# A chunked gated recurrence in 64x64 products: scores and results per 64 tokens, one masked copy for two heads, the state's part one step sooner

## The reference, cut to what matters

```
for each chunk of 64 tokens, each head:
    cum    = cumsum(log_f)                                   # per key channel
    scores[i,j] = sum_d q[i,d] k[j,d] exp(cum[i,d]-cum[j,d]) # j <= i, inside the chunk
    o      = scores @ v + (q * exp(cum)) @ state
    state  = exp(cum[last]) * state + (k * exp(cum[last]-cum))^T @ v
o = rmsnorm(o over the 64 values, norm_g) * silu(g)
```

## Time and profile before

| | |
|---|---|
| Median of 3 runs | 2164.09 us |
| Profiled execution, its own time | 2164.18 us |
| Its span | 2162.5 us |
| TensorE busy | 2140.3 us, 99% |
| VectorE busy | 1239.3 us, 57% |
| ScalarE busy | 914.9 us, 42% |
| GpSimd busy | 138.0 us, 6% |
| Pairs of the recurrence | 226 to 328 us of the span |

### The profile page before, as it was taken

The page is one execution under the profiler, slowest core; times in us unless marked ns, Lnnn a source line. Parts: engine busy times, 40 slices in busy tenths (PEclk is TensorE's granted clock), DMA queues, the critical chain, the costliest instruction groups (busy, mean ns, idle before and its releaser), DMA issues.

```text
span 2162.5 us, 26314 instructions
## 1 busy us (share of the span) xinstructions
PE 2140.3 (99%) x10412; PEld 1696.3 (78%) x10412; DVE 1239.3 (57%) x1835; ACT 914.9 (42%) x1449; POOL 138.0 (6%) x174
## 2 busy tenths in 40 slices
PE   9999999999999999999999999999999999999999
PEld 7768778678888888887777788888887667888887
DVE  5674784564554444474667555555556676555554
ACT  4464444554432332343555433333345555333332
POOL 0000332101000000020011000000021100000000
PEclk9999999999999999999999999999999999999999
DMA  4212112113222223222112222223221112232223
GB/s 175 86 49 88 49 45 93 47 59 127 98 98 98 91 96 106 97 88 88 50 59 68 88 98 98 97 98 98 98 88 59 59 40 89 97 104 96 94 98 107
DMA packets 52105, 187.04 MB, mean 86 GB/s; under 512 B 5904, under 2 KB 6032, under 8 KB 51856
## 3 DMA queue, kind: packets, MB, share of 16 engines
q1 hardware_dynamic: 51840, 185.18, 25.7%
q10 hardware_dynamic: 144, 0.18, 0.0%
HBM read 183.25 MB, written 2.10 MB: 86 GB/s over the span
## 4 chain that ended last, share of the span: by engine, by line
PE 92%; DVE 4%; ACT 2%; issue 1%; DMA 0%; SPq 0%; DVEq 0%; ACTq 0%
PE ps L1016 23%; PE ps L1019 23%; PE ps L1022 23%; PE ps L1040 4%; PE ps L1043 4%; PE ps L1041 4%; PE ps L995 3%; PE ps L1093 1%; PE ps L1145 1%; PE ps L1339 1%; PE ps L1357 1%; PE ps L1117 1%; PE ps L1163 1%; PE ps L1237 1%; DVE wl L1768 1%
## 5 line engine op out<-in xcount | busy, mean ns | idle before, releaser
L1416 ACT CAST wh<-raw 128x1024 fp32r<-128x1024 f32 x334 | 350.9, 1051 | 869.6 <-PE ps L1022 793.0
L1768 DVE TENSOR_TENSOR wl<-raw,wh 128x1024 fp32r<-128x1024 f32 (+2 forms) x338 | 414.7, 1227 | 174.9 <-ACT wh L1416 174.2
L1016 PE MATMUL ps<-hh,wh 128*128 128x512 f32 x1408 | 448.2, 399 | 2.5 <-ACT wh L1422 1.2
L1019 PE MATMUL ps<-hh,wl 128*128 128x512 f32 x1408 | 435.1, 390 | 2.4 <-DVE wl L1768 2.4
L1022 PE MATMUL ps<-hl,wh 128*128 128x512 f32 x1408 | 434.2, 390 | 0.0
L1019 PEld LDWEIGHTS ps<-hh,wl 128*128 128x128 f32 x1408 | 264.1, 188 | 59.6 <-DVE wl L1768 3.7
L1016 PEld LDWEIGHTS ps<-hh,wh 128*128 128x128 f32 x1408 | 257.5, 188 | 67.8 <-issue 15.9
L1022 PEld LDWEIGHTS ps<-hl,wh 128*128 128x128 f32 x1408 | 264.3, 188 | 56.4 <-DVE hl L1849 0.3
L1016 PE MATMUL ps<-R,wh 128*128 128x512 f32 x896 | 286.2, 400 | 0.0
L1019 PE MATMUL ps<-R,wl 128*128 128x512 f32 x896 | 277.4, 390 | 0.5 <-DVE wl L1768 0.5
L1022 PE MATMUL ps<-R,wh 128*128 128x512 f32 x896 | 276.9, 390 | 0.0
(11 more groups left out here) (226 smaller groups left out, 2030.9 us busy)
## 6 DMA issues: line engine op xcount, KB each, us to landing
raw<-in_weights SPq DMA_DIRECT2D x332, 512.0 KB, 3.4
x<-in_x_t SPq DMA_DIRECT2D x4, 512.0 KB, 7.0
F<-in_x_t SPq DMA_DIRECT2D x4, 512.0 KB, 5.0
out<-x SPq DMA_DIRECT2D x8, 256.0 KB, 2.0
raw<-in_weights SPq DMA_DIRECT2D x4, 416.0 KB, 3.2
x<-in_bias SPq DMA_DIRECT2D x1, 1024.0 KB, 7.5
F<-in_weights SPq DMA_DIRECT2D x2, 384.0 KB, 3.8
F<-in_weights SPq DMA_DIRECT2D x2, 256.0 KB, 5.1
```

Of the source, the lines that this page charges most:

```text
L1016: pe.matmul(out, hi[:, k, cs], B.tile(u.src, k)[0], start=k == 0, stop=False)
L1019: pe.matmul(out, lo[:, k, cs], B.tile(u.src, k)[0], start=False, stop=False)
L1416: act.copy(B.wh[s][:, 0:nk * ncol], B.raw[s][:, 0:nk * ncol]).then_inc(S["w_hi"], 1)
L1768: dve.tensor_tensor(lo, src, hi.bitcast(F32), ALU.subtract).then_inc(S[name], 1)
```

## The change

Keys and queries are now of the same 64 tokens. For each chunk c and each head there is one product of the 64 keys (stationary) by 64 queries (level 0) or 32. The even chunk of a pair of chunks goes to output partitions 0 to 63, the odd one to 64 to 127, each head to its bank. Sc shrinks from [2 heads, 512] to [2 heads, 256] columns, the masks to 32 columns, and one copy_predicated takes both heads. Results are products of 64 tokens' values with a 64x64 tile of Sc; even chunks lie in bank 6, odd ones in bank 7, in the first 256 columns. The mean squares go to the last 256 columns of the same two banks, as two products. State's part is a step of its own, `h_carry`, in step 6 behind level 6's scores; it opens the banks, and the results are added to it in step 7. The finishing operations read and write with the chunks' order (even, odd) changed by their patterns. Two constants that nothing used are gone, the first part of the constants is 256 columns smaller, and `h_zero` clears 512 columns and not 1024.

```diff
-CN = ["ident", "onesD", "negU", "negones", "bd64", "ones128"]
+CN = ["ident", "onesD", "bd64", "ones128"]
-NFIRST = 32 + 4 * P
+NFIRST = 32 + 2 * P
...
+                    if lv == 6:
+                        tick.append(("h_carry", p))
...
+    def h_result(self):
+        return self.two_banks(H_OUT[0])[:, :, 0:256]
+    def h_parts(self):
+        return self.V(3).rearrange("p (c t) -> p c t", c=2)
+    def h_squares(self):
+        return self.two_banks(H_OUT[0])[:, :, 256:512]
...
+H_OUT = (6, 7)
...
     def h_score(p, lv):
-            q, k, n = B.f4("F4")[:, p, :], B.f4("F2")[:, p, :], P
+            q, k, n = B.f4("F4")[:, p, :], B.f4("F2")[:, p, :], 64
...
-            q, k, n = B.h_queries(6 * p + lv - 1), B.h_keys(6 * p + lv - 1), 64
-        for tt in range(4):
+            q, k, n = B.h_queries(6 * p + lv - 1), B.h_keys(6 * p + lv - 1), 32
+        for c in range(8):
+            to, ts, qs = slice(64 * (c % 2), 64 * (c % 2) + 64), slice((c // 2) * n, (c // 2) * n + n), slice(c * n, c * n + n)
             for hf in range(2):
-                rr, qs = slice(64 * hf, 64 * hf + 64), slice(tt * n, (tt + 1) * n)
-                last = pe.matmul(two[hf][:, qs], k[rr, tt * P:(tt + 1) * P], q[rr, qs], start=True, stop=True)
+                rr = slice(64 * hf, 64 * hf + 64)
+                last = pe.matmul(two[hf][to, ts], k[rr, c * 64:c * 64 + 64], q[rr, qs], start=c < 2, stop=True,
+                                 skip_group_check=True)
...
+    def h_carry(p):
+        two = [empty(b) for b in H_OUT]
+        state, _ = B.k_state()
         at.wait_ge("hg_st", 7 * (p + 1))
         at.wait_ge("hg_tq", p + 1)
         for c in range(1, 8):
-            cs = slice(c * 64, (c + 1) * 64)
+            cs = slice((c // 2) * 64, (c // 2) * 64 + 64)
             for hf in range(2):
                 rr = slice(64 * hf, 64 * hf + 64)
-                last = pe.matmul(bank[rr, cs], state[rr, c, :], B.V(2)[rr, cs], start=False, stop=True,
+                last = pe.matmul(two[c % 2][rr, cs], state[rr, c, :], B.V(2)[rr, c * 64:(c + 1) * 64], start=c < 3, stop=False,
                                  skip_group_check=True)
+        last.then_inc(S["hg_i"], 1)
+
+    def h_out(p):
...
+        at.wait_ge("hg_i", p + 1)
+        at.wait_ge("hg_c", 7 * (p + 1))
+        for c in range(8):
+            rr, cs = slice(64 * (c % 2), 64 * (c % 2) + 64), slice((c // 2) * 64, (c // 2) * 64 + 64)
+            for hf in range(2):
+                h = 2 * p + hf
+                last = pe.matmul(B.bank[H_OUT[c % 2]][64 * hf:64 * hf + 64, cs], v4[rr, c // 2, h * 64:(h + 1) * 64],
+                                 Sc[rr, hf, c // 2, :], start=False, stop=True, skip_group_check=True)
         last.then_inc(S["hg_o"], 1)
-        emptied[7] = (("hg_d", 2 * p + 1),)
+        for b in H_OUT:
+            emptied[b] = (("hg_d", 2 * p + 1),)

     def h_ms(p):
-        bank = empty(6)
         at.wait_ge("hg_sq", p + 1)
-        pe.matmul(bank[:], B.const("bd64"), B.V(3), start=True, stop=True).then_inc(S["hg_ms"], 1)
-        emptied[6] = (("hg_r", 2 * p + 1),)
+        for i, b in enumerate(H_OUT):
+            last = pe.matmul(B.bank[b][:, 256:512], B.const("bd64"), B.V(3)[:, 256 * i:256 * i + 256], start=True, stop=True)
+            emptied[b] = (("hg_r", 2 * p + 1), ("hg_d", 2 * p + 1))
...
     def h_score(p, lv):                                        # VectorE
-        for hf in range(2):
-            bank = B.bank[h_pair(p, lv)[hf]]
...
-            last = dve.copy_predicated(to, mask, src)
-        last.then_inc(S["hg_c"], 1)
+        n = 32 if lv else 64
+        half, blocks = (64 >> lv, lv_blocks(lv) // 2) if lv else (64, 1)
+        src = B.two_banks(h_pair(p, lv)[0])[:, :, 0:4 * n].rearrange("p h (t b j) -> p h t b j", t=4, j=half)
+        mask = B.const(f"M{lv}", n).bitcast(U32).rearrange("p (b j) -> p b j", j=half).unsqueeze(1).unsqueeze(1)
+        mask = mask.to_broadcast([P, 2, 4, blocks, half])
...
+        dve.copy_predicated(to, mask, src).then_inc(S["hg_c"], 1)
...
-        pool.memset(B.F["F3"][:, 1024:2048], 0.0).then_inc(S["hg_z"], 1)
+        pool.memset(B.F["F3"][:, 1024:1536], 0.0).then_inc(S["hg_z"], 1)
```

More of the change, by code:

```diff
@@ L22 @@
 LAM_INIT = 0.8 - 0.6 * float(np.exp(-0.3))
-CN = ["ident", "onesD", "negU", "negones", "bd64", "ones128"]
+CN = ["ident", "onesD", "bd64", "ones128"]
 CX = {"eps": 0, "one": 1, "invA": 2, "invB": 18}
 CX.update({n: 32 + i * P for i, n in enumerate(CN)})
-NFIRST = 32 + 4 * P
-CX.update({f"M{lv}": 32 + len(CN) * P + 64 * (lv - 1) for lv in range(1, 7)})
-CX["AQ"] = 32 + len(CN) * P + 6 * 64
+NFIRST = 32 + 2 * P
+CX.update({f"M{lv}": 32 + len(CN) * P + 32 * (lv - 1) for lv in range(1, 7)})
+CX["M0"] = 32 + len(CN) * P + 6 * 32
+CX["AQ"] = CX["M0"] + 64
 CX["AK"] = CX["AQ"] + P
@@ L47, in const_array @@
     put("onesD", np.full((P, P), 1.0 / D))
-    put("negU", -1.0 * (a >= b))
-    put("negones", np.full((P, P), -1.0))
     put("bd64", same / 64.0)
@@ L54, in const_array @@
         half = blk // 2
-        pairs = (a // blk == b // blk) & (a % blk < half)
-        put(f"M{lv}", pairs.reshape(P, -1, 2, half)[:, :, 1, :].reshape(P, 64))
+        pairs = ((a % 64) // blk == b[:, 0:64] // blk) & (a % blk < half)
+        put(f"M{lv}", pairs.reshape(P, -1, 2, half)[:, :, 1, :].reshape(P, 32))
+    put("M0", a % 64 == b[:, 0:64])
     put("AQ", -1.0 * (same & (a <= b)))
@@ L876, in k_state @@
         s = self.F["F3"]
-        return s[:, 0:512].rearrange("p (c v) -> p c v", c=8), s[:, 1024:2048].rearrange("p (h t) -> p h t", h=2)
+        return s[:, 0:512].rearrange("p (c v) -> p c v", c=8), s[:, 1024:1536]
     def c_parts(self):
@@ L1240, in h_score @@
             emptied[b] = (("hg_c", 7 * p + lv + 1),)
[L1242 to L1248, removed]
-            for hf in range(2):
-                h = 2 * p + hf
-                pe.matmul(bank[64 * hf:64 * hf + 64, ts], v4[:, tt, h * 64:(h + 1) * 64], Sc[:, hf, ts],
-                          start=tt == 0, stop=True, skip_group_check=True)
+    def h_carry(p):
+        two = [empty(b) for b in H_OUT]
+        state, _ = B.k_state()
         at.wait_ge("hg_st", 7 * (p + 1))
@@ L1255, in h_out @@
         for c in range(1, 8):
-            cs = slice(c * 64, (c + 1) * 64)
+            cs = slice((c // 2) * 64, (c // 2) * 64 + 64)
             for hf in range(2):
                 rr = slice(64 * hf, 64 * hf + 64)
-                last = pe.matmul(bank[rr, cs], state[rr, c, :], B.V(2)[rr, cs], start=False, stop=True,
+                last = pe.matmul(two[c % 2][rr, cs], state[rr, c, :], B.V(2)[rr, c * 64:(c + 1) * 64], start=c < 3, stop=False,
                                  skip_group_check=True)
+        last.then_inc(S["hg_i"], 1)
+    def h_out(p):
+        _, Sc = B.k_state()
+        v4, Sc = B.f4("F0"), Sc.rearrange("p (h t j) -> p h t j", h=2, j=64)
+        at.wait_ge("hg_i", p + 1)
[6 more added lines that the diff above has]
+                                 Sc[rr, hf, c // 2, :], start=False, stop=True, skip_group_check=True)
         last.then_inc(S["hg_o"], 1)
-        emptied[7] = (("hg_d", 2 * p + 1),)
+        for b in H_OUT:
+            emptied[b] = (("hg_d", 2 * p + 1),)
     def h_ms(p):
-        bank = empty(6)
         at.wait_ge("hg_sq", p + 1)
-        pe.matmul(bank[:], B.const("bd64"), B.V(3), start=True, stop=True).then_inc(S["hg_ms"], 1)
-        emptied[6] = (("hg_r", 2 * p + 1),)
+        for i, b in enumerate(H_OUT):
+            last = pe.matmul(B.bank[b][:, 256:512], B.const("bd64"), B.V(3)[:, 256 * i:256 * i + 256], start=True, stop=True)
+            emptied[b] = (("hg_r", 2 * p + 1), ("hg_d", 2 * p + 1))
+        last.then_inc(S["hg_ms"], 1)
     def c_turn(j):
@@ L1643, in h_sq @@
         at.wait_ge("hg_o", p + 1)
-        act.activation(B.V(3), B.bank[7][:], ACT.Square).then_inc(S["hg_sq"], 1)
+        act.activation(B.h_parts(), B.h_result(), ACT.Square).then_inc(S["hg_sq"], 1)
     def h_ms(p):
@@ L1648, in h_ms @@
         at.wait_ge("hg_ms", p + 1)
-        act.activation(w, B.bank[6][:], ACT.Ln, bias=eps, scale=1.0).then_inc(S["hg_r"], 1)
+        act.activation(B.h_parts(), B.h_squares(), ACT.Ln, bias=eps, scale=1.0).then_inc(S["hg_r"], 1)
         at.wait_ge("hg_r", 2 * p + 1)
@@ L1654, in h_low @@
         at.wait_ge("hg_d", 2 * p + 2)
-        act.copy(B.R[2][:, p * T:(p + 1) * T], B.V(3)).then_inc(S["yb_h"], 1)
+        to = B.R[2][:, p * T:(p + 1) * T].rearrange("p (t c j) -> p t c j", c=2, j=64)
+        act.copy(to, B.h_tokens()).then_inc(S["yb_h"], 1)
     def c_sq(tt):
@@ L2154, in h_score @@
         at.wait_ge("hg_s", 7 * p + lv + 1)
-        for hf in range(2):
-            bank = B.bank[h_pair(p, lv)[hf]]
[L2157 to L2165, removed]
-            last = dve.copy_predicated(to, mask, src)
-        last.then_inc(S["hg_c"], 1)
+        n = 32 if lv else 64
[3 more added lines that the diff above has]
+        mask = mask.to_broadcast([P, 2, 4, blocks, half])
+        if lv:
```

(14 more changed lines are left out.)

6 lines of the change are left out of this document (4 added, 2 removed).

## The result

The changed kernel takes 2149.12 us (median of 4 runs, 2149.01 to 2149.40) against 2164.11: 15.0 us less, a ratio of 0.9931 with the interval 0.9919 to 0.9942. The forecast was 2150.0, so the time was right to 0.9 us. Its two terms were not: TensorE's products gave 15.3 us where 11.2 were counted, and TensorE's waits gave nothing where 2.9 were counted.

The account below looks back on a forecast made before the run. TensorE's stream was taken to bound the kernel. Its products (-11.2 us) and its waits for VectorE (-2.9) sum to -14.1, from 2164.09 to 2150.0 us; range given 2145.5 to 2157.5, the forecast's own 2147 to 2152.5.

Parts of the forecast that it names:

- Scores, 21.8 ns a record, 0.70 a group: Score groups at levels 1 to 6: 32 records at the state's update's price, 1.04 to 0.70 us, 8.2 us less.
- Level 0 and results, 0.70: Level 0's score groups and the result groups each fall from 1.09 to 0.70 us, 1.6 us less for each kind.
- The mean square, +0.1: One 512-column product becomes two of 256; 0.03 us added for each of four, 0.1 in all.
- Masked copies: One VectorE copy for both heads, 0.42, 0.65 or 0.73 us; 15 us in all, 13 less, counting only through stalls.
- Stalls, -2.9: TensorE's waits for VectorE: all 2.2 us of the results' go, and 0.7 of the scores' 1.5.
- State's part a step sooner: State's part moves behind level 6's scores, putting its 0.96 us ahead of the results' wait for the copy.
- The added wait of bank 6: The next pair's cumulated sums wait for VectorE's first finishing operation; some 0.6 us of margin remain, costed at nothing.
- A: Rival: a floor of 25 to 30 ns per record in score and result groups; 2153 to 2158 us; chance 0.17.
- C: Rival: no gain from the quarters, 34 ns a record; 2162 to 2163 us, no change that can be told; chance 0.06.
- D: Rival: weight loads follow one another at 65 ns a record in score and result groups; slower, 2194 us; chance 0.03.
- B: Rival: the time follows the query columns, 8.4 us more gain; down to 2141.6 us; chance 0.08.
- E: Rival: the stalls stay, as VectorE's bunches move with TensorE, or the new wait bites; 2153 to 2156 us; chance 0.06.

Follow-up runs that it names:

- `wide_keys`: The changed kernel with score products of 128 keys by the new number of queries, 8 a group, every second chunk's scores left out: 2158.14 us.
- `copies_tiny`: The changed kernel with each level's masked copy cut to one element, scores left out of the result: 2148.37 us.
- `low_late`: The changed kernel with the high and low part of a pair's result moved from step 3 of the next pair to step 7: 2146.30 us.
- `carry_late`: The changed kernel with state's part back in the step of the results, ahead of them: 2150.20 us.
- `halves_outer`: The changed kernel with score products ordered even chunks first, then odd, so two quarters of the array take turns: 2154.61 us.
- `carry_banks`: The changed kernel with state's part written to one bank per head instead of one per parity of the chunk: 2149.13 us.
- `copies_twice`: The changed kernel with every masked copy done twice, the first time into a spare region: 2155.17 us.

## Why the prediction was right, point by point

- *What bounds it.* Right: TensorE's stream sets the time, and the 15.1 us of its pieces in this stretch are the 15.0 of the kernel.
- *Scores, 21.8 ns a record, 0.70 a group.* Mis-sized: 0.60, with 14.4 ns for each further record, outside the 20 to 24 ns of my own range. Term -8.2, measured -10.6. I divided 0.61 us by 28 records although the piece holds a fixed part of 0.12 to 0.14 us, paid once by a run of groups in one tiling: the state's update behind scores of another tiling is 0.61, behind scores of its own 0.49. But that slip is worth only 0.02 us a group: 0.12 + 32 x 0.49/28 = 0.68. The other 0.08 is that a record of the row I borrowed from costs more than a score's (0.49/28 = 17.5 ns, unless a fixed part is left in the 0.49). It is not the 64 columns or the order of the quarters alone, for the results have both and take 0.62 for 32 records; the cause stays open. The Trainium skill, "TensorEngine Tiling (Array Packing)", section "Key Properties", says that changing the tiling mode drains the engine; the traces fit that, with 0.12 us, which `wide_keys` brings back for both groups behind it.
- *Level 0 and results, 0.70.* The same mistake: 0.62, -3.8 where -3.2 was counted.
- *State's part and the state's update.* I cost their change at nothing; each lost a change of tiling, -1.0 together.
- *The mean square, +0.1.* The products cost nothing more, 0.86 as before, but one of four waits 0.38 us for ScalarE's square and takes 1.07: +0.2, by a wait that I had not counted.
- *Masked copies.* Right: 15.80 us against the 15 worked out, 0.42 to 0.46 coarse, 0.72 to 0.74 fine (0.65 was said), 0.74 at level 0. That they are cheap was needed: doubled, they cost 6.0 us, 3.4 of waits and the rest by the clock.
- *Stalls, -2.9.* This step failed. The results' waits did go (-2.2). But I took half of the scores' 1.5 us off by setting VectorE's gain per step against TensorE's; TensorE came 0.44 us earlier per step and not 0.34, and what stood ahead of all three weightings was a split of weights, ahead of the longest also a wait for ScalarE, which the change doesn't touch. They grew to 3.7. That the faster products brought them is shown by the runs that only slow the scores down: with 0.85 us a group the scores' waits for VectorE are 2.1 to 2.2 us, with 1.01 they are 0.7 and with 1.06 they are 0.6. `copies_tiny` shows that the copies are not their cause (2.8 us remain), and `low_late` that what stands ahead in the queue is (0.7 remain). TensorE waits of over 2.5 us in this stretch were my own sign of a wrong forecast, and 3.7 is over it.
- *State's part a step sooner.* Counted as cover for the copy's wait. `carry_late` shows that no cover was needed, and that the move carried 1.1 us by another mechanism: state's part and results no longer stand back to back.
- *The added wait of bank 6, the constants, GpSimd's clearing.* Nothing seen, as said: no wait of the sums appears.
- *The two rules of the Trainium skill.* The Trainium skill's page "TensorE: Matmul & The Clock Gate", section "Wait — 56ns, not 53.3ns?", has a floor of about 25 ns from start to start. Taken per record, as I took it, it would have given -10.9, and the 14.4 ns of a further record lie under it; per product, which leaves two records, it is 28.8 ns and over it, and no run here tells which of the two the page counts. The warning about a dimension that is already small, which I set beside it, did not apply: the tiling is taken from the 128 key columns, not from the 32 query columns. The Trainium skill's page "TensorEngine Tiling (Array Packing)", section "Gotcha 1: PSUM Pressure", says that different row tiles can't write one PSUM bank at the same time. By it I put the new groups in the right class, for a reason that the runs do not bear out: in `halves_outer` each half of the rows has its own bank and the group is slow all the same, and in `carry_banks` giving each its own changes nothing. For the scores it is the number of quarters that take turns.
- *Rivals.* A, C and D are refuted by the 0.60 group, though D's and C's fear, tiles that wait for each other, is real for another order (0.85). B had the larger gain but not the reason: 64 columns cost 0.62 and 32 cost 0.60. E's mechanism held in full, the stalls stayed, though its times (2153 to 2156) did not. The forecast's time came out right by luck: two errors of 4.1 and 2.9 us went opposite ways. Either alone would have left the 2147 to 2152.5 given for the forecast's own mechanism (2145.9 or 2152.9), but not the wider range.

## What to carry to other kernels

Price a group of small products by two groups of different length, in the order and with the neighbours that they will have, and not by dividing another one: here the quotient said 21.8 ns a record where a further record costs 14.4. When an engine on the chain gets faster, go along the other engines' queues at the waits and read what stands ahead of the awaited instruction, idle times in that queue too; a lighter load elsewhere in the queue helps it little (0.75 us for a VectorE busy 63 us and not 71), a moved operation does (2.8 us for 0.69). And lay products whose results are added to each other so that others lie between (0.26 us a pair here).

## What the runs showed of the hardware that was not expected

- In 64x64 products of float32, the order of the quarters counts: in the scores a record costs 14.4 ns with all four in turn and 22 with two, whether the two share their rows or their output partitions.
- With 64 rows by 128 stationary columns a group of 16 records takes 1.01, 1.04 and 1.09 us for 32, 64 and 128 moving columns, 63 to 68 ns a record with the fixed part in it.
- A change of tiling between two groups costs 0.12 us: the state's update takes 0.61 us behind scores of another tiling (before, `wide_keys`) and 0.49 behind its own.
- In `copies_twice` the granted clock read 0.57 over 4 us, twice, after waits of 2.07 and 1.97 us with small products behind them, and the dense products that followed took 1.7 times as long. The changed kernel, whose longest wait in this stretch is 1.5 us, keeps 1.00.
